# A hybrid retention / RG-LRU / PEER step on one core: the head's closing gather piece moved behind the next head's rotation, retention products regrouped, an early load of seven merged heads

## The chip, the cores and the metric

The kernel runs on one core of one Trainium2 chip. The metric is device time in microseconds (us) of one execution, given as the median of several runs. Durations inside the kernel come from one profiled execution of the same program.

## The reference, cut to what matters

One layer on 1024 prompt tokens and 8 x 8 sample tokens, with 1024 channels. Per head (8 of them) there is a chunked retention, a convolution with an RG-LRU recurrence, and a gated sum of the two; `w_out` mixes the heads. Then PEER picks 128 experts for each token out of 16384 and gathers their rows.

```python
def step(S, inp):                                    # retention, chunks of 128 tokens
    qc, kc, vc = inp
    scores = jnp.einsum('bnhd,bmhd->bhnm', qc, kc) * mask
    o = (jnp.einsum('bhnm,bmhv->bnhv', scores, vc)
         + jnp.einsum('bnhd,bhdv->bnhv', qc, S) * xi[None, :, :, None])
    S = S * g_chunk[None, :, None, None] + jnp.einsum('bmhd,bmhv->bhdv', kc * zeta[None, :, :, None], vc)
    return S, o
...
merged = jax.nn.sigmoid(gate_a) * ret_out + jax.nn.sigmoid(gate_b) * lru_out
x = x + g1 * (merged @ w_out)
...
def blk(args):                                       # PEER, 128 tokens at a time
    xb, eb, gb = args
    act = jax.nn.gelu(jnp.einsum('td,tkd->tk', xb, u_tab[eb]))
    return jnp.einsum('tk,tkd->td', gb * act, v_tab[eb])
```

## The kernel before, in words

Data lie with channels on partitions and tokens in the free dimension. The tokens are treated in two halves. Half A (`zA`) holds the first 256 prompt tokens and the 64 sample tokens, half B (`zB`) the other 768 prompt tokens in six chunks of 128. The big tile `W` is shared by nearly everything of the mixer, so most rows of the profile name `W` and have to be told apart by their line. The code has names for parts of it (`z.qT`, `z.osb`, `hn2T`, `wo`).

A loop over the eight heads runs once for A (in the first 450 us) and once for B (from about 582 us to 1328 us of the span). Its body is one function for each engine, and the engines meet only at semaphores: `mix_sync` on SP (weight loads for the next head, stores), `mix_scalar` on ACT, `mix_tensor` on PE, `mix_vector` on DVE.

For head f of half B the order is as follows. PE projects the head's queries, keys and values one head ahead (`qkv_tiles`, L901), and ACT copies them out. DVE rotates queries and keys (the rotation, L1096 to L1100), which releases `rope_ready`, scales the keys for the state (`kz`, L1103), and then, once ACT has copied the convolution's input out (`xr_ready`), does the convolution (L1113, L1117). PE runs five projections (`part`, L930) and between them the transposes of rotated queries and keys (L959, they wait for `rope_ready`), the state products (`kv`, L966), the scores (L974), the two LRU gates (`lru_gate`, L938), the retention outputs (`outp`, L1008 and L1010) and the mean and the variance of each head (L1027). These small products share two PSUM banks `R[0]` and `R[1]` in turn (`stage_wait`): a product can start only when the one two places before it has been read by DVE or ACT. DVE reads the state products (L1157) and the scores (L1168). Its last operations in a head are L1257, L1258 and L1259, which leave the merged head in `z.osb` and release `mg_ready`; SP stores it to DRAM (L784).

While DVE does half B it also does the first part of PEER. `fill` takes the next step of a plan written out by hand: some pieces of a top-k search (L1716 and after) and two to four jobs, each a dot product of a gathered row with the token's row (L1779, about 1.2 us) or, from job 320 on, a weighted sum (L1789, about 1.3 us). The rows come by indirect DMAs that POOL issues (L1577) into a ring of six places. A head of half B has 14 fills, which take all 112 steps in eight heads; for half A `fill` does nothing. The fourteenth fill of a head stands at the very end of `mix_vector`, after `mg_ready`. Between heads 3 and 4 DVE also waits for POOL's last candidate products and makes their indices (L1673), and ahead of head 7 it normalizes the weights of the picks.

In the last head PE multiplies by `w_out` what is stored so far (`mixed_low`, L704) and adds the last head from SBUF (`mixed_high`, L711). DVE adds that to the residual (`residual(1)`, L1635). `mixed(2)` (L2297) then does the next 256 tokens from a copy of all eight merged heads read back from DRAM (`mg_load`, L686); its destination `hn2T[2]` lies over tiles of half B that are free once `mg_ready` has come.

The piece of `outp` that the change touches, for one group of chunks (`quad` is chunks 0 to 3 or 4 and 5 in half B):

```python
for n, c in enumerate(range(*quad)):
    first = z.sample and c == 0
    mm = pe.matmul(r[:, n * P:(n + 1) * P], z.tok[:, c, P:2 * P], z.pT[:, c, :], start=True, stop=first)
    if not first:
        mm = pe.matmul(r[:, n * P:(n + 1) * P], z.Sall[:, c, :], z.qxi[:, c * P:(c + 1) * P], start=False, stop=True)
```

`z.tok` and `z.pT` have 128 partitions, `z.Sall` and `z.qxi` have 64. Each product of float32 operands is two matmul instructions in the profile.

Of the kernel before, what the change touches and what calls it, by code (L numbers as in the profile page):

```python
# [27 lines left out]
P = 128  # L28
# [8 lines left out]
H = 8  # L37
# [228 lines left out]
def program(nc, I, O, S):  # L266
# [3 lines left out]
    def sem(name):  # L270
        return ctx.enter_context(nc.semaphore(name))
# [24 lines left out]
    with ctx:  # L296
# [115 lines left out]
        def w_in_load(sp, f, j):  # L412

            a, b = (0, CW) if j == 0 else (CW + (j - 1) * P, CW + j * P)
            dst = w_qkv if j == 0 else w_part[j - 1]
            src = I["w_in"][bass.ds(f, 1), :, a:b].rearrange("o (k p) n -> p (o k) n", p=P)
            sp.dma_start(dst[:, :, :], src).then_inc(w_in_sems[j], 16)

        def wab_load(sp, f):
            for q in range(2):  # L420
                src = I["wax"][bass.ds(f, 1), 64 * q:64 * q + 64].rearrange("o p a e -> p (o a) e")
                sp.dma_start(wab[64 * q:64 * q + 64, :, 64 * q:64 * q + 64], src).then_inc(wab_in, 16)

        def s0_load(sp, f):
            src = I["state_ret"][bass.ds(f, 1)].rearrange("o p n -> p (o n)")
            sp.dma_start(S0[:, :, :].rearrange("p b v -> p (b v)"), src).then_inc(S0_in, 16)

        def slab_load(sp, f):
            src = I["w_ada"][:, bass.ds(f * ADA_W + len(EARLY) * ADA_W, ADA_W)].rearrange("(k p) n -> p k n", p=P)
            sp.dma_start(ada_late[:, :, :], src).then_inc(ada_in[0], 16)  # L430
# [245 lines left out]
        mg_in, mg_first = [sem(f"mg_in{i}") for i in range(2)], sem("mg_first")  # L676
        o2_ready = sem("o2_ready")

        def x_load(sp, g):
            c0, n = XG[g]  # L680
            sp.dma_start(x2T[g][:, :, 0:n], I["xT"][:, c0:c0 + n].rearrange("(k p) t -> p k t", p=P)).then_inc(x_in[g % 2], 16)

        def mg_load(sp, g, h0, h1, landed):
            n = XG[g][1]
            src = S["mga"] if g == 0 else S["mgb"][:, :, (g - 1) * GT:g * GT]
            sp.dma_start(hn2T[g][:, h0:h1, 0:n], src[h0:h1].rearrange("f p t -> p f t")).then_inc(landed, 16)  # L686

        def wo_load(sp, j):

            ks = slice(0, 2) if j == 0 else slice(j + 1, j + 2)  # L690
            sp.dma_start(wo[:, ks, :], I["w_out"].rearrange("(k p) n -> p k n", p=P)[:, ks, :]).then_inc(wo_in if j < 6 else ada_in[0], 16)
# [37 lines left out]
        def weights_used(sp, z, f, j):  # L729

            if j % 2 == 0 and j:
                sp.wait_ge(pk_ready, f * 4 + (4 * z.base + j // 2 + 1))
            elif j == 5:
                sp.wait_ge(pk_ready, f * 4 + (4 * z.base + 4))
            else:
                sp.wait_ge(pj_ready, f * 5 + (5 * z.base + (j + 3) // 2))

        def gates_used(sp, z, f):
            sp.wait_ge(pj_ready, f * 5 + (5 * z.base + 5))

        def mix_sync(sp, z, f, last):

            b = z.base
            if last:
                if z.sample:
                    sp.wait_ge(mg_out, 16 * (b + H - 1))
                    mg_load(sp, 0, 0, H - 2, mg_first)
                for j in range(5):
                    weights_used(sp, z, f, j)
                    wo_load(sp, j)  # L750
            if not last:
                for j in range(6):
                    weights_used(sp, z, f, j)
                    w_in_load(sp, f + 1, j)
                gates_used(sp, z, f)
                wab_load(sp, f + 1)
                if z.sample:
                    sp.wait_ge(slab_row, f + 1)
                    slab_load(sp, f + 1)
            sp.wait_ge(S_ready, f + (b + 1))  # L760
            dst = (S["st"] if z.sample else O["ret_prompt"])[bass.ds(f, 1)].rearrange("o k v -> k (o v)")
            sp.dma_start(dst, z.Sall[:, z.nt, :]).then_inc(st_out, 16)
            if z.sample:
                sp.wait_ge(Sout_ready, f + 1)
                sp.dma_start(O["ret_sample"][bass.ds(f, 1)].rearrange("o p n -> p (o n)"), Sout[:, :, :].rearrange("p b v -> p (b v)")).then_inc(st_out, 16)
            if not last:
                sp.wait_ge(S0_used, f + (b + 1))
                if z.sample:
                    s0_load(sp, f + 1)
                else:  # L770
                    carry_load(sp, f + 1)
            else:
                g = 0 if z.sample else 1
                weights_used(sp, z, f, 5)
                if not z.sample:
                    mg_load(sp, g, 0, LOW_K, mg_first)
                wo_load(sp, 5)
                sp.wait_ge(mg_out, 16 * (b + H))
                mg_load(sp, g, H - 2 if z.sample else LOW_K, H - 1, mg_in[g])
                gates_used(sp, z, f)  # L780
                wo_load(sp, 6)
                x_load(sp, g)
            sp.wait_ge(mg_ready, f + (b + 1))
            sp.dma_start(S["mga" if z.sample else "mgb"][bass.ds(f, 1)].rearrange("o p t -> p (o t)"), z.osb[:, :]).then_inc(mg_out, 16)  # L784

        def carry_load(sp, f):
            sp.dma_start(zB.Sall[:, 0, :], S["st"][bass.ds(f, 1)].rearrange("o k v -> k (o v)")).then_inc(S0_in, 16)
# [123 lines left out]
        def mix_tensor(pe, z, f, last):  # L911
# [31 lines left out]
            def stage_wait():  # L943

                n = st[0]
                if n < 2:
                    pe.wait_ge(var_free, f + (b + 1))
                else:
                    pe.wait_ge(st_free, f * z.nst + (z.sf0 + n - 1))
                st[0] += 1  # L950
                return R[n % 2]
# [51 lines left out]
            def outp(quad):  # L1003
                r = stage_wait()
                pe.wait_ge(pT_ready, f + (b + 1))
                for n, c in enumerate(range(*quad)):
                    first = z.sample and c == 0
                    mm = pe.matmul(r[:, n * P:(n + 1) * P], z.tok[:, c, P:2 * P], z.pT[:, c, :], start=True, stop=first)  # L1008
                    if not first:
                        mm = pe.matmul(r[:, n * P:(n + 1) * P], z.Sall[:, c, :], z.qxi[:, c * P:(c + 1) * P], start=False, stop=True)  # L1010
                mm.then_inc(st_ready, 1)

            def outp_s():
# [69 lines left out]
        def mix_vector(v, z, f, fill):  # L1083

            b, fs, n = z.base, bass.ds(f, 1), z.cols
            st = [0]

            def stage():
                st[0] += 1
                v.wait_ge(st_ready, f * (z.nst + z.nvar) + (z.st0 + st[0]))  # L1090
                return R[(st[0] - 1) % 2]
# [14 lines left out]
                                      szeta[:, fs, :].rearrange("p o b -> p (o b)").unsqueeze(2).broadcast_to([TS, NB, DK]), ALU.mult)  # L1106
            ins.then_inc(kz_ready, 1)

            v.wait_ge(xr_ready, f + (b + 1))
            if z.sample:  # L1110
                xls = seqs(z.xl[:, FIRST:TA], NS)
# [15 lines left out]
            if z.sample:  # L1127
                r = stage()
                v.tensor_copy(z.qT[:, 0:FIRST], r[0:DK, 0:FIRST]).then_inc(st_free, 1)
                r = stage()  # L1130
                v.tensor_scalar(z.kT[:, 0:FIRST], r[0:DK, 0:FIRST], DK ** -0.5, None, ALU.mult).then_inc(st_free, 1)
                r = stage()
# [17 lines left out]
            for lo, hi in z.quads:  # L1150
                r = stage()
# [14 lines left out]
            for lo, hi in z.quads:  # L1166
                r = stage()
# [5 lines left out]
            if z.sample:  # L1173
                r = stage()
# [11 lines left out]
            if z.sample:  # L1186
                r = stage()
# [4 lines left out]
                r = stage()  # L1192
# [3 lines left out]
                r = stage()  # L1196
# [8 lines left out]
            if z.sample:  # L1205
                v.wait_ge(mg_out, f * 16 + (16 * b + 16))
                r = stage()
                v.tensor_copy(z.osb[:, 0:FIRST], r[:, 0:FIRST]).then_inc(st_free, 1)
                r = stage()
# [16 lines left out]
            for i, (lo, hi) in enumerate(z.slices):  # L1226
                r = stage()
# [31 lines left out]
            v.tensor_tensor(z.osb, z.osb, z.glru, ALU.add).then_inc(mg_ready, 1)  # L1259
            v.wait_ge(mg_ready, f + (b + 1))  # L1260
            v.sem_inc(f_done, 1)
            fill()

        with nc.Block() as block:
            @block.sync
# [155 lines left out]
        def x2_begin(g):  # L1421
            return 8 * g + (1 if g > SG else 0)
# [12 lines left out]
        with nc.Block() as block:  # L1435
            @block.sync
            def _(sp):
# [49 lines left out]
                with sp.Fori(0, H - 1) as f:  # L1487
                    mix_sync(sp, zB, f, False)
# [2 lines left out]
                sp.dma_start(O["lru"], lruo[:, :, :]).then_inc(lo_out, 16)  # L1491
                sp.wait_ge(st_out, 32 + 48 * H)
                sp.wait_ge(mg_out, 16 + 32 * H)
                mg_load(sp, 2, 0, H, mg_in[0])
                for j in range(16, 20):
                    wq_load(j)
                sp.wait_ge(o2_ready, x2_end(1))
# [789 lines left out]
            def _(pe):  # L2287
# [2 lines left out]

                def mixed(g):

                    pe.wait_ge(mg_in[g % 2], 32)
                    for m in range(KC):
                        pe.wait_ge(x2_ready, x2_begin(g - 1) + 2 * (m // 2) + 2)
                        for k in range(KC):
                            mm = pe.matmul(vacc[:, m, :], wo[:, k, m * P:(m + 1) * P], hn2T[g][:, k, 0:GT], start=(k == 0), stop=(k == KC - 1))  # L2297
                        mm.then_inc(o2_ready, 1)
# [196 lines left out]
                for g in range(NDG):  # L2495
                    last = g == NDG - 1
# [14 lines left out]
                for k in range(KC):  # L2511
                    mm = pe.matmul(tps[:, k * TS:(k + 1) * TS], spare[:, k * P:(k + 1) * P], sel, start=True, stop=True)
# [3 lines left out]
                for k in range(KC):  # L2516
                    mm = pe.matmul(nps[:, 0:TS], ones[:, :], sqb[:, 0:2, :].rearrange("p a t -> p (a t)")[:, k * TS:(k + 1) * TS], start=(k == 0), stop=(k == KC - 1))
# [66 lines left out]
```

## Time and profile before

| | us |
|---|---|
| median of 3 runs | 3552.17 |
| lowest and highest | 3543.63, 3560.54 |
| the profiled execution's own time | 3544.39 |
| its span, first to last instruction | 3542.6 |
| half B's heads, first rotation to last `mg_ready` | 582.7 to 1327.7 |
| the mixing of the later tokens and their PEER queries | from 1327.7 |

Engine names: PE is TensorE, PEld its weight loads, DVE VectorE, ACT ScalarE, POOL GpSimd, SP SyncE. "PEclk" is the granted TensorE clock as a share of full speed. "issue" in a chain of waits is time in which the engine waited for nothing that the profile shows; a wait of PE that stands in front of a `hold` is put down so.

### The profile page before, as it was taken

Reading aid. Unit: us, or ns where it says so; the run is one execution under the profiler, and the core shown is the slowest. Engines: PE = TensorE matmul, PEld = TensorE weight load, DVE = VectorE, ACT = ScalarE, POOL = GpSimd, SP = SyncE. Lnnn points to the kernel's source line nnn. Section 1 sums busy time; section 2 is a strip of 40 time slices with the busy share of each in tenths; the row PEclk is TensorE's granted clock in tenths of the full one; section 3 lists DMA queues with packets and bytes.
Section 4 is the critical chain, followed back from the end, with each engine's and each line's share of the span. In section 5 each row is a group of like instructions: output and inputs, shape, how many; then the busy total and the mean of one; then the engine's idle time right before and its main releaser. Section 6 shows DMA issues by size and latency. Waiting matters only on the chain.

```text
span 3542.6 us, 58071 instructions
## 1 busy us (share of the span) xinstructions
PE 3215.9 (91%) x18410; PEld 2578.3 (73%) x18410; DVE 2752.7 (78%) x5883; ACT 1385.5 (39%) x3099; POOL 1912.4 (54%) x1504
## 2 busy tenths in 40 slices
PE   7999999999999988988999999999999999998665
PEld 4777766666666667877788888878877788877554
DVE  3333356898889887789899999989999887667766
ACT  4444311222232221487555555555555565000110
POOL 0000013565566664344767777767766676676775
PEclk9999999999999999999999999999999999999899
DMA  8444454778889999678999999999999999999998
GB/s 266 148 148 148 141 166 149 251 251 265 266 292 335 326 343 324 233 259 297 380 392 396 380 383 401 365 360 399 391 353 384 372 405 407 389 410 407 400 404 344
DMA packets 429309, 1127.33 MB, mean 318 GB/s; under 512 B 41952, under 2 KB 166240, under 8 KB 429152
## 3 DMA queue, kind: packets, MB, share of 16 engines
q0 software_dynamic: 204800, 745.10, 56.1%
q1 hardware_dynamic: 219584, 370.51, 29.3%
q10 hardware_dynamic: 4768, 9.96, 0.7%
q8 instruction: 57, 0.93, 0.1%
q14 instruction: 100, 0.82, 0.1%
HBM read 1098.82 MB, written 26.62 MB: 318 GB/s over the span
## 4 chain that ended last, share of the span: by engine, by line
PE 35%; DVE 18%; DMA 16%; issue 14%; POOL 4%; ACT 1%; POOLq 0%; ACTq 0%; DVEq 0%; SPq 0%
PE vacc L930 11%; DMA rows<-in_peer_u,eidx 10%; PE vacc L2383 7%; DVE rows L1779 7%; PE vacc L901 5%; PE scat L2317 4%; DMA rows<-in_peer_v,eidx 4%; POOL rows L1577 3%; DVE oh1w L1860 2%; PE vacc L2297 2%; DVE oh L1855 1%; POOL W L1577 1%; DVE eidx L1673 1%; DMA W<-in_peer_v,eidx 1%; DVE htok L1789 1%
## 5 line engine op out<-in xcount | busy, mean ns | idle before, releaser
L1577 POOL DMA_INDIRECT rows<-in_peer_u,eidx x1072 | 1380.6, 1288 | 909.7 <-DVE dots L1779 557.7
L1779 DVE CUSTOM_DVE_ANT_0 rows<-rows,htok 128x1024 f32<-128x1024 f32 x1072 | 1327.1, 1263 | 156.6 <-DMA rows<-in_peer_u,eidx 146.1
L2383 PE MATMUL vacc<-W,vbuf 128*128 (+1 forms) x6144 | 1420.3, 386 | 30.3 <-DMA vbuf<-in_peer_v 21.3
L2383 PEld LDWEIGHTS vacc<-W,vbuf 128*128 128x128 f32 x6144 | 1153.3, 192 | 179.1 <-issue 31.4
L2117 ACT ACTIVATE oh<-iota,e2s 128x128 bf16<-128x128 f32 x1536 | 486.5, 391 | 16.3 <-DVE wpart L1831 9.4
L930 PE MATMUL vacc<-W 128*128 128x384 f32 x1280 | 434.4, 495 | 1.2 <-ACTq L803 1.2
L1556 POOL TENSOR_TENSOR hot<-hot,ccid 128x864 f32<-128x864 bf16 x68 | 130.5, 1923 | 531.5 <-DVE hot L1764 530.2
L930 PEld LDWEIGHTS vacc<-W 128*128 128x128 f32 x1280 | 242.1, 193 | 167.8 <-issue 8.6
L2124 ACT ACTIVATE W<-scat 128x256 f32 (+1 forms) x320 | 122.9, 384 | 569.4 <-PE scat L2370 566.2
L2120 ACT ACTIVATE oh<-oh,ones 128x512 bf16<-128x512 bf16 x384 | 277.2, 722 | 12.5
L1860 DVE TENSOR_TENSOR oh1w<-oh,wpart 128x768 bf16<-128x768 bf16 x384 | 241.3, 628 | 34.9 <-PE vacc L2370 16.4
L2317 PE MATMUL scat<-W 128*128 128x256 f32 (+1 forms) x1024 | 251.1, 401 | 5.4 <-DVE W L1657 5.4
L2370 PEld LDWEIGHTS scat<-oh1w,oh 128*128 128x128 bf16 x3840 | 155.5, 97 | 104.4 <-issue 55.3
L2317 PEld LDWEIGHTS scat<-W 128*128 128x128 f32 x1024 | 195.1, 195 | 44.8 <-issue 7.3
L2370 PE MATMUL scat<-oh1w,oh 128*128 128x64 bf16 x3840 | 167.6, 192 | 47.9 <-DVE oh1w L1860 41.2
L1577 POOL DMA_INDIRECT rows<-in_peer_v,eidx x138 | 156.5, 1134 | 57.6 <-issue 36.6
L1789 DVE SCALAR_TENSOR_TENSOR htok<-rows,dots,htok 128x1024 f32<-128x1024 f32 x104 | 133.6, 1285 | 67.6 <-DMA rows<-in_peer_v,eidx 65.9
L930 PE MATMUL vacc<-rows,W 128*128 128x320 f32 x640 | 179.8, 436 | 2.4 <-ACTq L803 2.4
L901 PE MATMUL vacc<-W 128*128 128x256 f32 x768 | 169.9, 382 | 0.0
L901 PEld LDWEIGHTS vacc<-W 128*128 128x128 f32 x768 | 147.0, 192 | 23.4 <-ACTq L868 1.9
L930 PEld LDWEIGHTS vacc<-rows,W 128*128 128x128 f32 x640 | 119.0, 190 | 53.3 <-ACTq L803 5.6
L1577 POOL DMA_INDIRECT W<-in_peer_v,eidx x118 | 130.5, 1106 | 44.1 <-issue 32.3
(347 smaller groups left out, 3316.4 us busy)
## 6 DMA issues: line engine op xcount, KB each, us to landing
vbuf<-in_peer_v SPq DMA_DIRECT2D x384, 512.0 KB, 6.8
W<-in_w_in SPq DMA_DIRECT2D x80, 512.0 KB, 6.6
W<-in_wq SPq DMA_DIRECT2D x64, 512.0 KB, 4.3
vbuf<-in_w_ada SPq DMA_DIRECT2D x9, 2048.0 KB, 8.1
rows<-in_peer_u,eidx POOLq DMA_INDIRECT x1072, 7.9
W<-in_w_in SPq DMA_DIRECT2D x16, 1024.0 KB, 6.4
W<-in_w_ada SPq DMA_DIRECT2D x3, 2048.0 KB, 16.1
W<-in_w_out SPq DMA_DIRECT2D x12, 512.0 KB, 7.1
```

Of the source, the lines that this page charges most:

```text
L901: mm = pe.matmul(dst, z.hnT[:, k, t * P:(t + 1) * P], w_qkv[:, k, :], start=(k == 0), stop=(k == KC - 1))
L930: mm = pe.matmul(pslice(z, pj if bank == "pj" else pk, s), w_part[j - 1][:, k, :], z.hnT[:, k, lo:hi], start=(k == 0), stop=(k == KC - 1))
L1556: g.tensor_tensor(h4, hotb[:, t].rearrange("p a n b -> p a b n"), cid[:, t, :].unsqueeze(1).unsqueeze(1).broadcast_to(shp), ALU.mult).then ...
L1577: g.indirect_dma_start(row_of[s], None, table[:, :], bass.IndirectOffsetOnAxis(ap=picked, axis=0)).then_inc(landed[s], 16)
L1779: v.tensor_tensor_reduce(row_of[s], row_of[s], htok[:, home, :], 1.0, 0.0, ALU.mult, ALU.add, dots_of(t)[:, c:c + 1]).then_inc(used, 1)
L1789: v.scalar_tensor_tensor(acc[t], row_of[s], w[:, c:c + 1], acc[t], ALU.mult, ALU.add).then_inc(used, 1)
L1860: v.tensor_tensor(oh1w[:, h, :, :, :, :], bc(oh1[:, j % EB, :, :, :], 1, shp), bc(wpart[:, u * QB + j, :, :, :], 3, shp), ALU.mult).then_i ...
L2117: ins = act.activation(oh2[:, h, n, :], iota[:, :], ACT.Abs, bias=e2s[:, bass.ds(k, 1)], scale=-1.0)
L2120: act.activation(oh2[:, h, :, :], oh2[:, h, :, :], ACT.Relu, bias=ones[:, 0:1], scale=-1.0).then_inc(oh2_ready, 1)
L2317: mm = pe.matmul(scat[u][:, 0:n], wq[j % 4][:, k, :], hn2T[g][:, k, 0:n], start=(k == 0), stop=(k == KC - 1))
L2370: mm = pe.matmul(banks[h][:, n * HK:(n + 1) * HK], oh2[:, h, n, :], oh1w[:, h, j, n // 2, :, n % 2], start=(j == 0), stop=(j == 2), skip_g ...
L2383: mm = pe.matmul(vacc[:, k, :], vbuf[:, s, k * P:(k + 1) * P], W[:, e1, :].rearrange("p o t -> p (o t)"), start=(clear and s == 0 and k % ...
```

## The change

Three edits. In half B the fill that closed a head (fourteenth) now stands in the head itself, between `kz` and the wait for `xr_ready`; the plan's order is the same, and each head still takes 14 steps. In `outp` all products of values come first, then all products of states; only the first product of a bank carries `start`, and the rest add to the cleared bank. The read-back for `mixed(2)` is split: heads 0 to 6 are loaded right behind the last head's store is issued, head 7 alone where all eight were loaded before, and `mixed(2)` waits for both.

```diff
@@ mix_sync
             sp.wait_ge(mg_ready, f + (b + 1))
             sp.dma_start(S["mga" if z.sample else "mgb"]..., z.osb[:, :]).then_inc(mg_out, 16)
+            if last and not z.sample:
+                mg_load(sp, 2, 0, H - 1, mg_in[0])
@@ outp
                 for n, c in enumerate(range(*quad)):
                     first = z.sample and c == 0
-                    mm = pe.matmul(r[...], z.tok[:, c, P:2 * P], z.pT[:, c, :], start=True, stop=first)
-                    if not first:
-                        mm = pe.matmul(r[...], z.Sall[:, c, :], z.qxi[...], start=False, stop=True)
+                    mm = pe.matmul(r[...], z.tok[:, c, P:2 * P], z.pT[:, c, :], start=(n == 0), stop=first, skip_group_check=True)
+                for n, c in enumerate(range(*quad)):
+                    if c or not z.sample:
+                        mm = pe.matmul(r[...], z.Sall[:, c, :], z.qxi[...], start=False, stop=True, skip_group_check=True)
                 mm.then_inc(st_ready, 1)
@@ mix_vector
             ins.then_inc(kz_ready, 1)
 
+            if not z.sample:
+                fill()
             v.wait_ge(xr_ready, f + (b + 1))
...
             v.wait_ge(mg_ready, f + (b + 1))
             v.sem_inc(f_done, 1)
-            fill()
@@ SP, after half B
                 sp.wait_ge(st_out, 32 + 48 * H)
                 sp.wait_ge(mg_out, 16 + 32 * H)
-                mg_load(sp, 2, 0, H, mg_in[0])
+                mg_load(sp, 2, H - 1, H, mg_in[0])
@@ PE, mixed(g)
-                    pe.wait_ge(mg_in[g % 2], 32)
+                    pe.wait_ge(mg_in[g % 2], 48 if g == 2 else 32)
```

## Rows read from the trace of the kernel before

**Rows 1.** The page: each engine's busy time and its share of the span.

```profile
PE 3215.9 (91%) x18410; PEld 2578.3 (73%) x18410; DVE 2752.7 (78%) x5883; ACT 1385.5 (39%) x3099; POOL 1912.4 (54%) x1504
```

**Rows 2.** Waits of PE, 600 to 1400: total us, times, longest.

```profile
PE scat L959 <- issue: 21.0, 5, 6.7
```

**Rows 3.** Chain that ended last, in time: start, us, what.

```profile
686.33 6.65 issue
692.98 1.46 PE scat L959 x6
694.44 7.46 PE vacc L930 x16
...
876.74 2.45 issue
...
1152.76 0.65 PE scat L959 x6
1153.41 5.16 PE vacc L930 x16
...
1240.67 2.69 issue
```

**Rows 4.** Windows: length, PE, PEld, DVE, ACT, POOL busy, PEclk, DMA, GB/s.

```profile
693.00:702.00 9.00, 9.00 (x25) 5.44 (x26) 7.65 (x20) 2.21 (x4) 1.84 (x2) 0.67 0.46 172
...
1061.60:1149.50 87.90, 87.90 (x334) 58.83 (x333) 79.09 (x132) 25.96 (x32) 59.06 (x49) 1.00 0.95 333
```

**Rows 5.** Timeline of DVE round the change of heads 0 to 1.

```profile
683.28 0.96 DVE L1259 TENSOR_TENSOR W<-W 128x768 f32<-128x768 f32 x1
...
690.00 0.95 DVE L1096 TENSOR_TENSOR W<-W 128x768 f32<-128x768 f32 x1
...
691.92 0.96 DVE L1100 TENSOR_TENSOR W<-W 128x768 f32<-128x768 f32 x1
```

**Rows 6.** Waits of DVE, 690.0 to 1327.75: total us, times, longest.

```profile
DVE rows L1779 <- DMA rows<-in_peer_u,eidx: 19.5, 25, 2.5
DVE x L1221 <- ACT x L874: 12.9, 5, 5.7
DVE W L1144 <- ACTq L815: 10.9, 7, 2.8
DVE htok L1789 <- DMA rows<-in_peer_v,dots: 5.7, 7, 1.8
...
DVE eidx L1673 <- POOL hot L1556: 2.8, 1, 2.8
```

**Rows 7.** Waits of DVE, 596 to 690.

```profile
DVE W L1113 <- ACT scr L288: 9.7, 1, 9.7
```

**Rows 8.** Chain of waits again, the small products of head 1.

```profile
714.67 1.09 PE scat L974 x8
...
736.70 0.42 PE scat L1008 x2
```

**Rows 9.** Timeline of DVE, head 1: reading the state products.

```profile
709.48 1.46 DVE L1157 SCALAR_TENSOR_TENSOR W<-W,scat 64x128 f32<-64x128 f32 x4
```

**Rows 10.** Timeline behind the last head.

```profile
1326.77 0.96 DVE L1259 TENSOR_TENSOR W<-W 128x768 f32<-128x768 f32 x1
1327.94 5.25 DVE L1789 SCALAR_TENSOR_TENSOR htok<-rows,rss,htok 128x1024 f32<-128x1024 f32 x4 [0.21 <-DVE W L1259]
1329.36 3.62 PE L711 MATMUL vacc<-W 128*128 128x256 f32 x16
1333.14 0.39 SPq L686 DMA_DIRECT2D W<-scratch_mgb  x1
1343.95 6.31 PE L2297 MATMUL vacc<-W 128*128 128x256 f32 x20 [10.97 <-DMA W<-scratch_mgb]
```

**Rows 11.** DMA issues of 1290 to 1325: KB each, us to landing.

```profile
W<-scratch_mgb SPq DMA_DIRECT2D x1, 512.0 KB, 15.1
W<-scratch_mgb SPq DMA_DIRECT2D x1, 384.0 KB, 7.4
```

More of the change, by code:

```diff
@@ L1007, in outp @@
                     first = z.sample and c == 0
-                    mm = pe.matmul(r[:, n * P:(n + 1) * P], z.tok[:, c, P:2 * P], z.pT[:, c, :], start=True, stop=first)
-                    if not first:
-                        mm = pe.matmul(r[:, n * P:(n + 1) * P], z.Sall[:, c, :], z.qxi[:, c * P:(c + 1) * P], start=False, stop=True)
+                    mm = pe.matmul(r[:, n * P:(n + 1) * P], z.tok[:, c, P:2 * P], z.pT[:, c, :], start=(n == 0), stop=first, skip_group_check=True)
+                for n, c in enumerate(range(*quad)):
+                    if c or not z.sample:
+                        mm = pe.matmul(r[:, n * P:(n + 1) * P], z.Sall[:, c, :], z.qxi[:, c * P:(c + 1) * P], start=False, stop=True, skip_group_check=True)
                 mm.then_inc(st_ready, 1)
```

## Prediction, made before the changed kernel was run

> **What bounds the kernel now.** I read the page first, to see which engines could matter at all. PE is busy 91% of the span and DVE 78% [rows 1], so neither is idle enough to be ignored, and an average cannot say which one a given stage waits for. The change touches half B's eight heads and the step behind them, so the second view was the chain of waits of that stretch. It runs on PE without a break through heads 0 to 6, except for pieces called "issue" in front of the transposes L959, such as 6.65, 2.45 and 2.69 us [rows 3]: 21.0 us in five of the seven changes of head [rows 2]. The transposes wait for `rope_ready`, and the timeline of DVE shows what is late. DVE ends the merged head at 684.24, does the closing fill, and starts the rotation only at 690.00; PE has been ready since 686.33 and starts at 692.98, when the rotation's sum is done [rows 3, 5]. So 5.8 us of top-k pieces and dot products stand between two links of PE's chain.
>
> The gap costs more than its length. Behind the 6.65 us gap the granted clock was 0.67 of full speed for 9 us, a stretch partly on the 1.2 GHz level [rows 4], and six transposes and sixteen projections took 1.46 and 7.46 us, against 0.65 and 5.16 in head 6, which had no gap [rows 3]: 3.1 us more. Without a gap a head takes PE 87.9 us, all busy, at full clock [rows 4].
>
> The third view was DVE's waits, since removing PE's gap only helps as far as DVE keeps up. From the start of rotation 1 to the last `mg_ready` (690.00 to 1327.73, 637.7 us [rows 5, 10]) DVE waits 12.9 + 10.9 us for ACT, which follows PE, and 2.8 us for POOL's products: 26.6 us. Another 25.2 us are waits for gathered rows, which an earlier PE does not shorten [rows 6]. That is all the slack the stage has. In the last head the bound changes: the chain leaves PE behind the gap at 1240.67, and DVE has hardly a wait for another engine there. Last, behind the last head, PE's `mixed(2)` starts at 1343.95, after an 11.0 us wait for the read-back from DRAM. It starts 16.2 us after `mg_ready`: 5.3 until the store has landed and the load is issued at 1333.14, and 10.8 for the load [rows 10].
>
> **The fill behind the rotation.** No work is added or removed: each head still does 14 fills. The rotation starts right after `mg_ready`, and `rope_ready` comes 2.9 us later. In head 0 the moved fill lies in a 9.7 us wait for ACT's copy [rows 7] and costs nothing; its cover is gone only if that wait were under the fill's 5.8 us. Head 0 ends about 1 us earlier, because `outp` is shorter (below): rotation 1 starts at 683.5 in place of 690.0, and PE's gap there is about 1 us, not 6.65. From then on PE would need 87.9 us a head and DVE its own work. What DVE needs from there to the last `mg_ready` is 637.7 less the 26.6 us of waits that an earlier PE and a later DVE close, plus one fill, because the closing fill of head 7, 5.25 us [rows 10], was behind `mg_ready` and now is in front of it: 616.4 us. So DVE sets the end: 683.5 + 616.4 = 1299.9. PE alone would be ready sooner (six heads of 86.7 from about 686, then the 86.0 from 1243.36 to mixed_high at 1329.36: about 1292). Two engines with so nearly the same load (DVE's heads need 85 to 89 us) don't hide every wait, and I add 2 us: 1302. That is 25.7 us earlier. Bounds of the term: all waits gone, 27.8; only half of the 26.6 gone, 14.5.
>
> What is queued behind the fill is the convolution, the query scaling L1144 and the reading of the state products L1157. DVE's waits for ACT go because DVE comes later to them. L1157 began 19.5 us behind the rotation's start in head 1 [rows 5, 9]; with 5.8 us more in front and 2.8 us of wait absorbed it begins at 22.5. The scores L974 need that bank: PE came to them at 24.7 [rows 8], but 3.1 us of that were low clock, so PE now comes at 21.6 and waits for L1157's end at 24.0. That is 2.4 us of new PE idle per head, inside a head in which PE has some 1 to 2 us to spare, and part of the 2 us I added.
>
> **Values first, states second.** In `outp` the pairs of instructions alternate between 128-row and 64-row weights and take 0.42 us a pair; the eight score instructions, all 64-row, take 1.09, 0.27 a pair [rows 8]. Six chunks are twelve pairs. Regrouped, three changes of kind are left of eleven: 12 x 0.27 + 3 x 0.15 = 3.7 us against 12 x 0.42 less the first pair's 0.2, 4.8 us, a gain of 1.1 to 1.2 us of PE per head. Its bounds are nothing and 12 x 0.15 = 1.8. Half A has one chunk without a state and one with, so its order is the same, and it gains nothing. In heads 1 to 7 DVE is the bound and the gain is only slack for PE; the whole edit is worth the 1 us in head 0.
>
> These rows contradict a rule that would speak against this edit. The Trainium skill, "TensorE: Matmul & The Clock Gate", section "LDWEIGHTS (loading the stationary operand)", says that a weight load of 32 rows takes as long as one of 128, so that the number of rows plays no part. By that rule the order of equal products is free and the edit brings nothing, and the forecast would be 1 us later; the pairs at 0.42 and 0.27 us do not agree with it.
>
> **The early load.** The store and the load of seven heads are now in the queue together, the load of head 7 follows the store's landing. SP issues one more DMA (0.4 us), ahead of two small stores, for which nothing waits; the loads of PEER's query weights and of the residual that stand behind the last piece in SP's queue are issued, as before, once the store has landed. From `mg_ready` the last piece has landed after 5.3 us of store and between 5.3 (the store's own time, a larger transfer) and 7.4 us (a 384 KB load of the same kind) [rows 10, 11]. The seven-head piece lands after 0.4 + 7/8 of 10.8 = 9.9 us if alone, and 15.1 if it fares like the 512 KB load that stood behind others in the queue [rows 11]. I take 12.7, by the nearest row: 3.5 us gained, with bounds 5.6 and 0.7. The closing fill no longer delays `residual(1)`, but that was not on the path.
>
> **The sum.** 25.7 + 3.5 = 29.2 us. Behind `mixed(2)` nothing hangs on absolute time: every engine is at the same place of its program, so the shift is carried to the end. The profiled execution would take 3544.4 - 29.2 = 3515.2. It lay 7.8 us below the median of the three runs, so the median becomes 3552.2 - 29.2 = 3523. POOL's queue of gathers is in the same order as before.
>
> **Rivals.**
> 1. *The forecast*, 3523. Its own range, from 14.5 + 0.7 to 27.8 + 5.6, is 3519 to 3537.
> 2. *Gathers take the place of DVE's waits.* DVE's idle time let the ring of six rows fill up. In heads 4 to 7 the DMA share is already 0.95 [rows 4], and if there each wait for ACT comes back as a wait for rows, the gain shrinks by it; with a third of the 23.8 us in these heads, 8 us, it is 25.7 - 8 + 3.5 = 21.2, hence 3531. Against it: only 25.2 us in seven heads are waits for rows [rows 6].
> 3. *The gap moves to the scores.* If the new 2.4 us wait lowers the clock as the gap of 2.45 us did, PE loses up to 3.1 us more, ACT's gates come some 2.1 us too late for DVE, and six heads give back 12.6 us: 29.2 - 12.6 = 16.6, hence 3536.
> 4. *Slower.* The same wait at the scores, but the low clock stays through the next projections. Sixteen projections at 1.2 GHz take twice 5.16 us [rows 3]; two such blocks in each of seven heads are 72 us, less 29 is 43 us slower, 3595. It decides from 4.2 us per head on (29.2 / 7), and ends beyond the bound of measurement from 6.7. For it speaks that PE is nearly always the chain; against it, that even behind the 6.65 us gap the whole low stretch cost 3.1 us.
> 5. *The change doesn't do what it says*: the transposes wait not for DVE but for something else that the profile calls "issue", and only the load's 3.5 us remain: 3549. The rotation's end and the transposes' start agree to 0.1 us, which speaks against it.
>
> **How the numbers follow.** Chances: forecast 0.64, gathers 0.13, scores 0.13, slower 0.05, no effect 0.05. A difference under 0.5% (17.8 us) can hardly be told from none for this kernel, so the border of "faster" is 3534. The forecast lies almost wholly under it, case 2 for two thirds, case 3 for a third: 0.62 + 0.09 + 0.04 = 0.75. Slower by more than that needs case 4: 0.05. The rest, 0.20, is within. The runs spread over 8 us to either side of the median, so I widen the forecast's range to 3508, and to 3545 for cases 2 and 3.
>
> **What would show it.** The pieces "issue" in front of L959 fall from 21 us to under 5, and no row of transposes takes 1.46 us. L1096 starts within 0.2 us of L1259's end. DVE's waits at L1221 and L1144 fall from 23.8 us to under 5. L1008 and L1010 take 3.7 us a head. L1259 of head 7 ends near 1302 and L2297 starts 12 to 13 us later. Wrong would be a wait of PE at L974 over 4 us or waits for rows over 35 us; the forecast fails if DVE's work is not the fixed amount that I took it for.

## The result

The changed kernel took 3526.01 us in the median of 12 runs (3509.23 to 3532.36), the kernel before 3545.53 us (12 runs, 3538.56 to 3560.54). The ratio is 0.9937, 95% interval 0.9925 to 0.995: 22 us less by the ratio, 19.5 by the medians, where 29 were forecast. The median forecast was 3523; that it lies only 3 us from the measured one is in part luck, since the kernel before came out at 3545.5 and not at the 3552.2 that the forecast started from. The profiled execution's span fell from 3542.6 to 3522.7 us. The line numbers of the changed kernel are higher: the rotation starts at L1099 (L1096 before), `mg_ready` is L1264, the transposes are L961, the scores L976, the values and states of `outp` L1010 and L1013, the dots L1783, `mixed(2)` L2301.

### The profile page after: what moved, and what is told of

Read it like the earlier page. It is cut to its first block, busy times and chain, and to the rows that moved or that the text cites. A ratio compares the mean times of both kernels' runs of the same rounds, so it can differ in the third digit from the quotient of the medians.

```text
span 3522.7 us, 58072 instructions
## 1 busy us (share of the span) xinstructions
PE 3209.1 (91%) x18410; PEld 2580.1 (73%) x18410; DVE 2750.3 (78%) x5883; ACT 1385.5 (39%) x3099; POOL 1930.7 (55%) x1504
## 3 DMA queue, kind: packets, MB, share of 16 engines
q1 hardware_dynamic: 219600, 370.51, 29.6%
## 4 chain that ended last, share of the span: by engine, by line
PE 19%; DVE 18%; issue 13%; DMA 11%; POOL 3%; ACT 1%; POOLq 0%; DVEq 0%; ACTq 0%; SPq 0%
PE vacc L2387 13%; DMA rows<-in_peer_u,eidx 7%; DVE rows L1783 7%; DVE oh1w L1864 2%; POOL rows L1581 2%; PE scat L2321 2%; PE vacc L2301 2%; DMA vbuf<-in_peer_v 2%; DMA rows<-in_peer_v,eidx 1%; DVE oh L1859 1%; DVE eidx L1677 1%; POOL W L1581 1%; PE scat L2374 1%; DMA W<-in_peer_v,eidx 1%; DVE ti L1728 1%
## 5 line engine op out<-in xcount | busy, mean ns | idle before, releaser
L1783 DVE CUSTOM_DVE_ANT_0 rows<-rows,htok 128x1024 f32<-128x1024 f32 x1072 | 1327.1, 1264 | 147.5 <-DMA rows<-in_peer_u,eidx 136.8
L2124 ACT ACTIVATE oh<-oh,ones 128x512 bf16<-128x512 bf16 x384 | 277.2, 722 | 12.5
```

The lines of the kernel that those rows point to most:

```text
L1783: v.tensor_tensor_reduce(row_of[s], row_of[s], htok[:, home, :], 1.0, 0.0, ALU.mult, ALU.add, dots_of(t)[:, c:c + 1]).then_inc(used, 1)
L2124: act.activation(oh2[:, h, :, :], oh2[:, h, :, :], ACT.Relu, bias=ones[:, 0:1], scale=-1.0).then_inc(oh2_ready, 1)
```

## The profile after

The waits of PE between 600 and 1400 us answer to [rows 2] (total us, times, longest):

```profile
PE scat L961 <- issue: 11.7, 4, 4.5
PE vacc L704 <- DMA W<-in_w_out: 6.8, 1, 6.8
PE vacc L711 <- DVE W L1264: 6.1, 1, 6.1
PE scat L976 <- DVEq L1168: 3.1, 2, 1.9
PE vacc L2301 <- DMA W<-scratch_mgb: 2.8, 1, 2.8
```

The gap at the transposes is 11.7 us, not 21.0 and not the "under 5" that was forecast. It stands ahead of heads 1, 4, 6 and 7 (2.4, 3.2, 1.7 and 4.5 us). New is 3.1 us at the scores, which wait for DVE to read the state products, and 6.1 us in front of the last head's product: PE now waits for DVE there. The longer of the two waits at the scores (1.9 us, head 3) follows a wait of DVE of 5.2 us for a block of token rows (`htok`, the last line of the next view) and not the moved fill.

The waits of DVE from rotation 1 to the last `mg_ready` (683.5 to 1311.6) answer to [rows 6]:

```profile
DVE rows L1783 <- DMA rows<-in_peer_u,eidx: 31.9, 41, 2.4
DVE htok L1793 <- DMA rows<-in_peer_v,dots: 6.1, 8, 2.0
DVE rows L1783 <- DMA htok<-scratch_hn: 5.2, 1, 5.2
```

No wait for ACT is left of 23.8 us, and none for POOL's products. The waits for gathered rows rose from 25.2 to 38.0 us. Nearly all of them lie in heads 4 to 7. There the kernel before (972.1 to 1327.75) and the changed kernel (950 to 1311.6) show, beside waits for the rows of `in_peer_v` of 5.7 and 6.1 us:

```profile
DVE rows L1779 <- DMA rows<-in_peer_u,eidx: 18.8, 24, 2.5
DVE W L1144 <- ACTq L815: 5.3, 4, 2.5
DVE x L1221 <- ACT x L874: 2.6, 2, 2.1
```

```profile
DVE rows L1783 <- DMA rows<-in_peer_u,eidx: 29.2, 38, 2.4
```

So in these four heads 7.9 us of waits for ACT went, and 10.8 us of waits for rows came. The windows of head 1 and head 6 (rotation to rotation; the columns are those of [rows 4]) show the two kinds of head:

```profile
683.50:771.60 88.10, 85.71 (x326) 57.49 (x325) 83.76 (x192) 26.32 (x32) 59.72 (x40) 0.98 0.82 262
1126.80:1215.70 88.90, 87.22 (x336) 58.55 (x335) 77.46 (x127) 26.33 (x35) 63.29 (x47) 1.00 0.95 328
```

Head 1 takes 88.1 us, of which DVE is busy 83.8, and none of its waits there is over 0.3 us: it is at its own pace. In head 6 DVE has 6 us less to do and still takes 88.9 us; 10.1 us of it are waits for rows.

The products of `outp` in head 1, in the timeline of PE, answer to [rows 8]:

```profile
725.78 1.05 PE L1010 MATMUL scat<-W 128*128 128x128 f32 x8
726.76 1.16 PE L1013 MATMUL scat<-W 64*128 64x128 f32 x8
727.85 0.71 PE L1010 MATMUL scat<-W 128*128 128x128 f32 x4
728.49 0.71 PE L1013 MATMUL scat<-W 64*128 64x128 f32 x4
729.12 5.43 PE L932 MATMUL vacc<-W 128*128 128x384 f32 x16
```

From 725.78 to 729.12 are 3.34 us for twelve pairs, 1.5 us less than the 4.9 before.

The timeline behind the last head answers to [rows 10]:

```profile
1310.62 0.96 DVE L1264 TENSOR_TENSOR W<-W 128x768 f32<-128x768 f32 x1
1311.61 0.35 SPq L784 DMA_DIRECT2D scratch_mgb<-W  x1
1311.64 5.81 PE L711 MATMUL vacc<-W 128*128 128x256 f32 x16 [6.11 <-DVE W L1264]
1312.00 0.44 SPq L686 DMA_DIRECT2D W<-scratch_mgb  x1
...
1317.05 0.34 SPq L686 DMA_DIRECT2D W<-scratch_mgb  x1
...
1320.24 1.99 PE L2301 MATMUL vacc<-W 128*128 128x256 f32 x8 [2.79 <-DMA W<-scratch_mgb]
```

`mg_ready` came at 1311.6, 16.1 us earlier, and `mixed(2)` began 8.6 us behind it, not 16.2. That makes 23.7 us at the start of `mixed(2)`. `mixed(2)` itself took 27.9 us in place of 29.6, after a shorter pause. The lead is then carried, 24 us where the bulk of the expert products starts (1656.3 against 1680.1), and 19.9 us at the end. Between these points no instruction differs. Over the 14 executions profiled for this document the time from the start of `mixed(2)` to the end was 2190.9 to 2206.5 us, so nothing is made of the last 4 us.

## Experiments

`mg_ready` below is that of head 7. Each ratio is against runs of the kernel before that were made beside it, so ratios are to be compared between experiments, and not medians.

**The fill alone.** The kernel before with only this edit:

```diff
             ins.then_inc(kz_ready, 1)
+            if not z.sample:
+                fill()
             v.wait_ge(xr_ready, f + (b + 1))
...
             v.sem_inc(f_done, 1)
-            fill()
```

> Only the fill is moved. Theory A (in the heads DVE's work plus its waits for rows sets the period; PE has slack): mg_ready of head 7 comes at 1311 to 1315, as in the changed kernel, although outp still takes 4.9 us a head; DVE waits for ACT fall under 3 us and waits for rows rise from 25 to 36 us or more; mixed(2) starts 16 us behind mg_ready; in all 13 to 16 us less than before. Rival B (PE sets the period once its gap is closed, so the regrouped products were worth 1.5 us in each of seven heads): mg_ready at 1320 or later, and about 7 us less than before in all.

Measured: median 3529.36, ratio 0.9947 (0.9927 to 0.9966), so nearly all of the gain. `mg_ready` came at 1319.9, and `mixed(2)` 11.7 us behind it and not 16, although the read-back was not split: it began 5.3 us after the load of all eight heads was issued, against 10.8 in the kernel before. The waits of PE, and then of DVE (690 to 1319.9):

```profile
PE vacc L2298 <- DMA W<-scratch_mgb: 7.9, 1, 7.9
...
PE scat L959 <- issue: 6.2, 5, 2.2
PE scat L974 <- DVEq L1165: 6.1, 5, 2.1
```

```profile
DVE rows L1780 <- DMA rows<-in_peer_u,eidx: 34.2, 31, 2.8
DVE htok L1790 <- DMA rows<-in_peer_v,dots: 6.5, 4, 2.4
DVE rows L1780 <- DMA htok<-scratch_hn: 5.5, 1, 5.5
DVE x L1223 <- ACT x L874: 3.6, 2, 1.9
```

The waits for rows are at 40.7 us, as theory A had it, but `mg_ready` lay at the border of B, 8.3 us later than in the changed kernel and 4.1 later than in its second execution (below). The gaps and the waits at the scores are 12.3 us together, against 14.8 in the changed kernel, and DVE waits for ACT again: with 4.9 us of `outp` a head PE is the slower one in some heads. Neither theory holds alone.

**The order alone.** The kernel before with `outp` regrouped (the diff of the change).

> Only the products of outp are regrouped. outp takes 3.3 us a head, not 4.9, in half B. Theory A: in the five changes of head where PE waits for the rotation the gap grows by what was saved, up to 1.5 us each, and the stage ends 2 to 5 us earlier (mg_ready 1323 to 1326). Rival B: the saving counts in every head, 8 x 1.5 = 12 us, mg_ready at 1316 and 12 us less in all.

Measured: median 3544.62, ratio 0.9988 (0.9974 to 1.0001); `mg_ready` at 1321.2, a gap of 23.7 us at the transposes against 21.0. The gap grew by 2.7 us, where 12 us of PE's work were saved. `mg_ready`, 6.5 us earlier in this one execution, lies between the two expectations, and the timed runs leave 0 to 9 us: a gain on its own can't be told from none.

**The load alone**, twice: the kernel before with the split read-back.

```diff
+            if last and not z.sample:
+                mg_load(sp, 2, 0, H - 1, mg_in[0])
...
-                mg_load(sp, 2, 0, H, mg_in[0])
+                mg_load(sp, 2, H - 1, H, mg_in[0])
...
-                    pe.wait_ge(mg_in[g % 2], 32)
+                    pe.wait_ge(mg_in[g % 2], 48 if g == 2 else 32)
```

> Only the read-back is split. mg_ready stays at 1327.7 within 1 us. From the changed kernel: mixed(2) starts 8.7 us behind it, not 16.2, and takes 28 us, not 30, because PE's pause before it is shorter: 9 to 10 us less in all. Rival (the short pause in the changed kernel owes to the closing fill that no longer delays the residual): mixed(2) starts 11 us or more behind mg_ready, 5 us less in all.

> The early load alone once more, since the profiled execution of the first lay 16 us above that kernel's own median. If the fill behind mg_ready is what slows the read-back (it frees four rows, and POOL fetches four more at once), mixed(2) again starts 13.5 to 14.5 us behind mg_ready, and not 8.6, and this kernel gains 2 to 4 us.

Measured: medians 3545.2 and 3543.9, ratios 0.9993 (0.9978 to 1.0009) and 0.9992 (0.9974 to 1.001). No gain can be told. `mixed(2)` began 14.0 and 12.0 us behind `mg_ready`, not 8.6; the second lies outside what was expected of it. DMA issues of the first of the two, 1340.9 to 1352 (KB each, us to landing):

```profile
W<-scratch_mgb SPq DMA_DIRECT2D x1, 896.0 KB, 10.4
...
W<-scratch_mgb SPq DMA_DIRECT2D x1, 128.0 KB, 8.0
...
rows<-in_peer_v,dots POOLq DMA_INDIRECT x4, 7.6
```

and of the changed kernel, 1311 to 1321:

```profile
W<-scratch_mgb SPq DMA_DIRECT2D x1, 896.0 KB, 7.1
...
W<-scratch_mgb SPq DMA_DIRECT2D x1, 128.0 KB, 3.1
...
rows<-in_peer_v,dots POOLq DMA_INDIRECT x1, 6.4
```

Where a fill stands behind `mg_ready`, DVE uses four rows, POOL sends four or five gathers (128 rows of 1024 float32 values, 512 KB each) beside the read-back, and the 128 KB piece takes 8.0 us, not 3.1. All executions agree: 6.7 to 8.1 us in the four with the split load and the fill behind `mg_ready` (the 6.7 is the second one here), 3.1 to 4.1 in the five with the split load and the fill ahead. In both executions of this kernel `mg_ready` itself lay at 1337 to 1341, 8 to 13 us behind that of the kernel before, with 32 to 37 us of waits for rows although DVE waited for ACT as long as before (26.4 and 24.0 us). No instruction ahead of it is different. That was not expected and is not explained, and it shows that waits for rows can grow by 7 to 12 us without any edit that touches them.

**The last fill behind `mg_ready` again**, in the changed kernel:

```diff
-            if not z.sample:
+            if not z.sample and f != H - 1:
                 fill()
...
             v.sem_inc(f_done, 1)
+            if not z.sample and f == H - 1:
+                fill()
```

> The changed kernel, but head 7 does its fourteenth fill behind mg_ready again, as the kernel before did. If the 5.3 us of that fill lie on the path in the changed kernel (DVE sets the end of head 7, PE waits 6.1 us for it), mg_ready comes at 1306, mixed(2) still starts 8.7 us behind it, because the residual that the fill delays ends before the read-back has landed: 5 us less than the changed kernel, ratio to before about 0.992. If the residual holds mixed(2) back, 3 us less or fewer.

Measured: median 3523.15, ratio 0.9918 (0.99 to 0.9936). `mg_ready` came at 1309.5, not 1306, and `mixed(2)` 14.4 us behind it, not 8.7. The 128 KB piece took 8.1 us to land; the residual was done 6 us before. So the fill costs on either side of `mg_ready`: ahead of it 5.3 us of DVE, behind it about as much through its gathers. `mixed(2)` began at 1323.9, between the two executions of the changed kernel (1320.2 and 1326.0). The timed runs would allow a small gain, but the intervals overlap.

**An order between the two** in `outp`, changed kernel:

```diff
-                for n, c in enumerate(range(*quad)):
...
-                for n, c in enumerate(range(*quad)):
...
+                for x in range(quad[1] - lo + 1):
+                    if x < quad[1] - lo:
...  # value x, then state x - 1
```

> The changed kernel with outp's products in the order V0 V1 S0 V2 S1 V3 S2 S3 (V values, S states): the kind of weights changes at nearly every product, as before the change, but no product adds to the columns that the one ahead of it has just written. If the change between 128-row and 64-row weights costs the time, a pair takes about 0.40 us and outp 4.3 to 4.8 us a head. If adding at once to the same columns costs it, a pair takes 0.27 us and outp 3.3 us, as in the changed kernel.

Measured: 3521.9 us in one run. The timeline of PE for head 1:

```profile
727.69 0.61 PE L1012 MATMUL scat<-W 128*128 128x128 f32 x4
728.23 0.49 PE L1015 MATMUL scat<-W 64*128 64x128 f32 x2
728.64 0.49 PE L1012 MATMUL scat<-W 128*128 128x128 f32 x2
729.06 0.48 PE L1015 MATMUL scat<-W 64*128 64x128 f32 x2
...
729.89 0.71 PE L1015 MATMUL scat<-W 64*128 64x128 f32 x4
```

The twelve pairs take from 727.69 to 731.81, 4.1 us. Pairs that alternate in kind start 0.41 to 0.42 us apart, as before the change, though none adds to the columns just written. So it is the change between 128-row and 64-row products that costs, not the adding to the same columns. Both operands change between 128 and 64 partitions here, and no run tells the weights from the other operand.

**A ring of ten rows** in heads 4 to 7, changed kernel:

```diff
+RING_LO, RING_HI, RING = 172, 340, 10
 def row_slot(n):
+    if RING_LO <= n < RING_HI:
+        k = (n - RING_LO) % RING
+        return (k + RING_LO) % VD if k < VD else k
     return n % VD if n < WIDE else (n - WIDE) % VW
...
+        def row_of(n):
+            s = row_slot(n)
+            return vbuf[:, s - VD, :] if n < WIDE and s >= VD else wide_row[s]
...
+                    if n == RING_LO + VD:
+                        g.wait_ge(idx_ready, H + NSU)
```

> The changed kernel with a ring of ten rows instead of six for jobs 172 to 339 (heads 4 to 7; the four more places lie in the buffer of expert rows, free then). Theory R (DVE waits for rows because only six gathers can be on their way, each some 8 us): its waits for rows in heads 4 to 7 fall from 35 us to under 12, and then PE or DVE's bare work sets the end, mg_ready at 1290 to 1297, 15 to 20 us less than the changed kernel. Rival C (the DMA engines are busy, and more gathers on their way only take longer each): waits for rows stay above 25 us and mg_ready at 1305 or later.

Measured: median 3504.32, ratio 0.9882 (0.9858 to 0.9905), the fastest kernel of this study. `mg_ready` at 1298.7, `mixed(2)` at 1308.4. Waits of DVE, 683.5 to 1298.7:

```profile
DVE rows L1795 <- DMA rows<-in_peer_u,eidx: 9.2, 9, 2.5
DVE x L1232 <- ACT x L882: 6.9, 4, 2.5
...
DVE W L1155 <- ACTq L823: 3.0, 1, 3.0
DVE vbuf L1795 <- DMA vbuf<-in_peer_u,eidx: 2.6, 5, 1.5
```

The waits for rows are 11.8 us, not 38.0, and waits for ACT are back (9.9 us): in heads 4 to 6 PE sets the pace now, with the chain of waits on PE alone there and 85 to 86.5 us a head. A gather took longer to land than with six places (median of the rows of `in_peer_u`, 950 us to `mg_ready`), and nearly the same bytes (119 and 118 MB) went through in less time:

```profile
rows<-in_peer_u,eidx POOLq DMA_INDIRECT x97, 7.3
```

```profile
950.00:1298.00 348.00, 335.97 (x1281) 226.54 (x1281) 320.79 (x494) 104.25 (x130) 252.87 (x192) 0.98 0.96 342
```

against 6.2 us and 328 GB/s in the changed kernel. In the last head DVE's `mg_ready`, the store and the read-back still end last, but PE, which waited 8.7 us for the last pieces of `w_out`, is only 0.8 us ahead of them:

```profile
1275.38 13.63 PE L710 MATMUL vacc<-W 128*128 128x256 f32 x48 [8.69 <-DMA W<-in_w_out]
...
1303.95 3.62 PE L717 MATMUL vacc<-W 128*128 128x256 f32 x16
1308.37 3.94 PE L2313 MATMUL vacc<-W 128*128 128x256 f32 x17 [0.79 <-DMA W<-scratch_mgb]
```

**Less weight traffic**, changed kernel. It leaves out seven of eight channel chunks of the next heads' projection weights in half B, which keep head 0's values.

```diff
...
-                    w_in_load(sp, f + 1, j)
+                    w_in_load(sp, f + 1, j, KC if z.sample else 1)
```

> The changed kernel, but in half B the next heads' projection weights are loaded for one of eight channel chunks only, the other seven keep head 0's values; 4 MB less of some 29 MB a head. Rival C (contention): waits for rows fall by a third or more, from 38 us to 25 or less, and mg_ready comes 10 us or more earlier than 1311.6. Theory R (number of gathers on their way): waits for rows change by less than 8 us.

Measured: median 3518.67, ratio 0.9925 (0.9905 to 0.9944); `mg_ready` at 1308.3, waits for rows 35.4 us (38.0 in the changed kernel). The DMA share of the last four heads fell from 0.94 to 0.87, the bytes moved there from 118 to 108 MB, and the waits hardly moved. That is theory R: traffic less by a twelfth doesn't help, four more places do. What a larger cut in traffic would do is not shown.

**Ring and last fill together**: the ring of ten in the changed kernel, and head 7's last fill behind `mg_ready`.

> The changed kernel with the ring of ten and with head 7's fourteenth fill behind mg_ready. If the ring works, the end of head 7 is PE's: its mixed_low and variance, about 1290; the fill behind is then worth 1 to 4 us more. In all 17 to 22 us less than the changed kernel, ratio to before about 0.988. If DVE keeps waiting for rows, it is 5 us less than the changed kernel.

Measured: median 3509.32, ratio 0.9897 (0.9876 to 0.9918). `mg_ready` at 1295.1, but `mixed(2)` at 1309.4, 14.3 us behind it, 1 us later than with the ring in the changed kernel. The ring's gain is there again; the fill behind brings no gain that can be told.

**The ring alone**, on the kernel before:

> The kernel before with the ring of ten for jobs 172 to 339 and nothing else. If the ring was a bound only once PE's gap was closed (the forecast's view: there DVE waited for ACT instead), its waits for rows fall from 25 us to 10 but the gaps at the transposes stay near 20 us, and mg_ready comes less than 6 us earlier. If waits for rows were already part of what made the rotation late, the gaps of heads 4 to 7 shrink too and mg_ready comes 10 us or more earlier.

Measured: median 3539.82, ratio 0.9984 (0.9967 to 1.0); `mg_ready` at 1330.2, no earlier than before. PE waits at the transposes, and DVE waits (690 to 1330.2):

```profile
PE scat L965 <- issue: 23.1, 6, 6.6
```

```profile
DVE x L1227 <- ACT x L880: 20.3, 6, 6.4
DVE W L1150 <- ACTq L821: 12.8, 6, 3.0
DVE rows L1791 <- DMA rows<-in_peer_u,eidx: 10.3, 13, 1.4
DVE vbuf L1791 <- DMA vbuf<-in_peer_u,eidx: 8.6, 7, 2.2
```

Waits for rows fell by 6 us, not by 15 as expected, and waits for ACT rose by 9. With the gap open, rows that come sooner only let DVE wait elsewhere.

**Both kernels once more.**

> The changed kernel once more, to see how much one profiled execution differs from another: if the stage is as regular as the two shown so far suggest, mg_ready of head 7 lies within 4 us of 1311.6, waits for rows within 5 us of 38.0, and mixed(2) starts 8.6 to 9.8 us behind it.

> The kernel before once more: mg_ready within 6 us of 1327.7, gaps at the transposes 19 to 26 us, mixed(2) 16 to 17 us behind mg_ready.

Measured: the changed kernel 3525.93 us in the median, ratio 0.9934 (0.9909 to 0.9958); `mg_ready` at 1315.8, waits for rows 39.9 us, `mixed(2)` 10.2 us behind. The kernel before 3541.23 us in one run; `mg_ready` at 1329.7, gaps 21.8 us, `mixed(2)` 16.1 us behind. So `mg_ready` moved by 2 to 4 us between executions of one program, the last interval by up to 1.6 us. The second pair has a lead of 13.9 us at `mg_ready`, 19.8 at the start of `mixed(2)` and 20.1 at the end, the first 16.1, 23.7 and 19.9.

**Where in the eight heads the time goes.** The traces hold a comparison that settles more than the sums over the stage. Taken from the ends of the operation that releases `mg_ready` (L1259 before, L1264 in the changed kernel), in us, one execution a row; from one head's `mg_ready` to the next each of these kernels does 14 fills, and the ring of ten works in heads 4 to 7 only:

| kernel | `mg_ready` of head 0 | heads 1 to 3 | heads 4 to 7 |
|---|---|---|---|
| before | 684.3 | 279.0 | 364.5 |
| before, again | 685.7 | 278.7 | 365.3 |
| changed | 683.5 | 266.0 | 362.1 |
| changed, again | 684.1 | 266.5 | 365.2 |
| the fill alone | 685.9 | 268.4 | 365.6 |
| the order alone | 682.4 | 271.5 | 367.3 |
| ring of ten alone | 685.4 | 278.7 | 366.1 |
| changed, with ring of ten | 686.3 | 266.6 | 345.8 |
| the load alone | 684.4 | 279.1 | 377.5 |
| the load alone, again | 686.6 | 277.2 | 373.7 |

The change gains 12 to 13 us in heads 1 to 3 and between nothing and 3 us in heads 4 to 7. In heads 4 to 7 two limits lie at nearly the same height: with ten places and the gap open the four heads take 366 us, with six places and the gap closed 362 to 365, and only with both removed 346. The timed runs agree: 0.0063 of the time for the change, 0.0016 for the ring, 0.0118 for both, with intervals of up to 0.0024 to either side. The unexplained delay of the load alone also lies in heads 4 to 7.

## Why the prediction came out as it did

The time (3526) lies in the range, and the sign and the mechanism of the gap were right; the gain was 22 us by the ratio where 29 were forecast. Of the prediction's own signs of being wrong one came true: waits for rows over 35 us (38.0 and 39.9). DVE's work was not the fixed amount that it was taken for.

- *PE waits for the rotation, and the rotation for the closing fill.* Right. In the changed kernel L1099 starts 0.1 us behind L1264's end in five of the seven changes of head; the fill alone brings 0.9947. Ahead of heads 4 and 7 DVE makes indices (L1677) or normalizes weights (L1691 and after) in between, 1.3 and 2.3 us, and two of the four gaps that are left, 3.2 and 4.5 us, stand there. The prediction also made DVE slower than PE by some 10 us and left PE under 5 us of gaps; where DVE is behind, PE waits for it, here or at the last head's product.
- *Head 0 hides the moved fill, rotation 1 at 683.5.* Right: 683.6. But PE's gap there was 2.4 us, not about 1.
- *DVE's waits for ACT go.* Right: 23.8 us to none. `mg_ready` should have come at 1302 and came at 1311.6.
- *DVE needs 637.7 - 26.6 + 5.3 = 616.4 us.* This is the term that was mis-sized. It took 628.1, 11.7 more, and the waits for rows took 12.8 more (38.0 for 25.2), with 1.8 more for the token rows. The prediction held them fixed, "which an earlier PE does not shorten"; they are not fixed. In heads 4 to 7 the ring of six holds the stage about where the gap had held it, so there the waits for ACT (7.9 us) were no gain to be had. That is the rival "gathers take the place", which priced it at 8 us with its "third of the 23.8 us"; the waits for rows in these heads rose by 10.8. The ring of ten takes most of it away (11.8 us of waits, `mg_ready` 12.9 us earlier), and a twelfth less traffic does not. That each wait of DVE for ACT had let the ring fill fits all this; it is not all of it, since the load alone showed 32 to 37 us of waits for rows with the waits for ACT in place. (The DMA share of 0.95 that the rival gives for heads 4 to 7 is that of head 5, the row it cites; over the four it is 0.85 to 0.95.)
- *The 2 us for two engines with the same load.* The fill alone suggests that PE's 1.5 us a head is not only slack: without it `mg_ready` is 4.1 and 8.3 us later than in the two executions of the changed kernel. "The whole edit is worth the 1 us in head 0" was too little by that; how much it is worth in the timed runs stays open, as 0.9947 and 0.9937 have overlapping intervals.
- *Scores wait 2.4 us a head.* There was none in head 1, for which it was worked out, because PE came later to them (23.4 us behind the rotation's start, not 21.6) behind its gap of 2.4 us and a clock of 0.72. In all it was 3.1 us in two heads, 7.0 in four in the second execution. The granted clock stayed at 1.00 in head 3, which had the longest of the first (1.9 us), so the rivals with a low clock did not happen. Low stretches are left where the gaps at the transposes are: 0.72 from 686 to 692, 0.76 from 953 to 960, 0.79 from 1220 to 1228. Behind the gap of 4.5 us ahead of head 7 six transposes took 1.46 us, which the prediction had ruled out.
- *`outp` at 3.7 us.* 3.34. Three changes of kind cost 0.1 us in all, not 0.45; seven of them cost 4.1 - 3.2 = 0.9 us in the order between. A change costs most where kinds alternate pair by pair. The rows didn't contradict the page of the Trainium skill itself, as the prediction says: one load takes as long for 64 rows as for 128 (last section). What they contradict is the step from there, that the order is free.
- *The read-back, 12.7 us behind `mg_ready`.* It was 8.6 to 10.2: the second term mis-sized, in the other direction. The last piece landed in 3.1 us, and 7.4 had been taken from a load among others in the queue. The prediction saw in the closing fill behind `mg_ready` only a delay of the residual, which was not on the path. The fill was on it through the gathers it sets off: with the old read-back but no fill there, `mixed(2)` came 11.7 us behind; with the new read-back and the fill, 12.0 to 14.4; with neither change 16.1 to 16.8; with both 8.6 to 10.2. Of the 6 to 8 us gained the split alone is 2 to 5 us and not measurable in the time.

Together: 25.7 + 3.5 = 29.2 forecast at the start of `mixed(2)`, 16.1 + 7.6 = 23.7 measured, 13.9 + 5.9 = 19.8 in the second pair. The first term was 10 to 12 us too high and the second 2 to 4 us too low; that they partly cancel is luck.

## What to carry to other kernels

Two limits can lie at the same height and hide each other: take the time of each stage apart by itself, try each remedy alone and both together, and don't drop one that brings nothing alone. Here the deeper ring was worth nearly as much again as the whole change (0.9882 against 0.9937), and next to nothing before the change was made (0.9984). So before counting all of an engine's waits for others as gain, ask which of its other waits may grow in their place. Work that is put beside a DMA on the path brings its own transfers along; look at what its completion sets free, not only at the engine that does it. And keep equal kinds of small products together, where PE is on the path.

## What the runs showed of the hardware

- Products of float32 operands with 128 columns (two instructions each) take 0.27 us in rows of one kind and 0.41 to 0.42 where products over 128 rows and over 64 rows alternate. Adding to the columns just written costs nothing more: 0.42 with it (the kernel before), 0.41 to 0.42 without (the order between). The Trainium skill, "TensorE: Matmul & The Clock Gate", section "LDWEIGHTS (loading the stationary operand)", gives the row count no part in a load's time. The trace agrees for a load alone: a median of 192 ns for 128 rows and 188 ns for 64. It is the change between kinds that costs here.
- With a ring of ten places a gather of 512 KB landed 7.3 us after its issue instead of 6.2, and the core moved 342 GB/s instead of 328 in the same heads: each took a little longer and the whole was faster.
- The read-back of 128 KB landed in 3.1 to 4.1 us where no gather had been issued in the 5 us before it, and in 6.7 to 8.1 us where four or five gathers of 512 KB stood beside it.
